# A hybrid decoder trunk: one weight quad loaded in halves, and state products put ahead of their additions

## The chip, the cores and the metric

The kernel runs on one core of a Trainium2 chip. The metric is device time in microseconds (us) of one execution. Before the change the median of 3 runs is 1538.26 us (1537.71 to 1540.48).

## What is computed

The reference runs one inference step of a two-layer trunk for a prompt (256 tokens) and for 8 samples of 8 tokens each that share the weights. A layer is a mixer (state-space heads beside retention heads), a cross-attention on 256 memory tokens, and a mixture of experts. The part that matters here is the mixer's carried state, and the projection of the memory for the attention that follows:

```python
def step(s, inp):                     # ssd_scan, one chunk: states of (heads, 64, 128) per sample
    cs, cd = inp
    return cd[..., None, None] * s + cs, s
y_off = jnp.einsum('bclgn,bcghpn,bclgh->bclghp', Cc, s_in, jnp.exp(a_cum))

def step(s, kv):                      # retention_chunkwise: states of (4, 128, 256) per sample
    return chunk_decay * s + kv, s
o_cross = jnp.einsum('bclhd,bchde->bclhe', q_start, s_in)

mem_k, mem_v = mem @ w_mk, mem @ w_mv # per layer, 256 tokens, 1024 to 1024
```

For the samples the old state s comes from memory, is multiplied by queries (y_off, o_cross), and a new state (decay times old state, plus a product of this step) is returned.

## The kernel before, in words

All weights and old states come through one stream of "quads", arrays of 128 partitions x 4096 floats (2 MB, 16 KB in each partition). SyncE (SP) issues their loads in a fixed order on one queue; each goes into a slot, and in the mixer there are three slots, called ring. A load waits until its slot is freed: `freed[s]` is raised by TensorE (riding on a later matmul) or by VectorE, `loaded[s]` by the landing.

The stage of the diff stands at the end of each layer's mixer. It takes four state quads, k = 0 to 3 (`Q_STATE`: retention, state space, retention, state space; four samples each), between which stand the four quads of memory weights (`Q_MEM`, 16 chunks of 128 columns, four to a quad). The order of the loads there is: second memory quad (chunks 4 to 7), state k = 1, state k = 2, third memory quad (chunks 8 to 11), state k = 3, fourth memory quad. The third memory quad goes into the slot of the second, state k = 3 into that of state k = 1.

TensorE's order is written out by hand. For each k: `from_states(k)` multiplies queries by old states (L860); `new_states(k, 0)` makes what is added to the first half of the new states (L893 for retention, L896 for state space); `project_memory(1)` does one chunk (L613, 16 matmuls); `turn_off(k)` transposes (L872) the result of from_states; then `new_states(k, 1)`. The banks of PSUM into which new_states writes are used again by each half, so a half waits for VectorE's addition of the half before (`s_newst`).

VectorE makes each new state half. For retention one instruction multiplies and adds (L1956). For state space there are two: old state times decay (L1962) and then the addition of the product from PSUM (L1969). Between the halves it scales what TensorE transposes (L1990, state space alone) and adds the transposed result (`add_off`, L1980; `s_offadd` releases from_states of the next k). After the second half it frees the state's slot. A gate product over the prompt (L2007) stands behind k = 0. GpSimd stores each half (1 MB) to memory from one of three buffers; `s_store` guards their reuse. ScalarE copies the memory chunks and the retention part out of PSUM.

Of the kernel before, what the change touches and what calls it, by code (L numbers as in the profile page):

```python
# [20 lines left out]
ALU = mybir.AluOpType  # L21
AX = mybir.AxisListType

P = 128
DEPTH = 2
D = 1024
KD = D // P
# [134 lines left out]
def build(nc, stream, params, consts, x_in, mem_in, y_out, st_out, conv_out, mk_out, mv_out):  # L162
    with ExitStack() as ctx:
# [150 lines left out]

        loaded = [sem(f"s_loaded{s}") for s in range(WIDER)]
        freed = [sem(f"s_freed{s}") for s in range(WIDER)]
        s_slab = [sem(f"s_slab{i}") for i in range(3)]
        s_sq = sem("s_sq")
        s_acc = sem("s_acc")
        s_acc0 = sem("s_acc0")  # L320
# [193 lines left out]
        @block.sync  # L514
        def _(sp):
            sp.dma_start(x[:], x_in).then_inc(s_const, 16)
            sp.dma_start(par[:], params.rearrange("l p n -> p l n")).then_inc(s_const, 16)
            sp.dma_start(cst[:, 0:FIRST], consts[:, 0:FIRST]).then_inc(s_const, 16)
            for L in range(DEPTH):
                for q in range(QUADS):  # L520
                    s, n = slot_of(q), use_of(L, q)
                    if n >= 1:
                        sp.wait_ge(freed[s], n)
                    if q == SLOTS.index(3):
                        for i in range(3):
                            sp.wait_ge(s_store[i], 16 * STORES[i] * (L + 1))
                    if q == SLOTS.index(4):
                        sp.wait_ge(s_ottout, (L + 1) * 4)
                        sp.wait_ge(s_mvstore, 16 * (L + 1))
                    if q == SLOTS.index(6):  # L530
                        sp.wait_ge(s_xs, L * 8 + 6)
                        sp.wait_ge(s_mkstore, 16 * (L + 1))
                    if q == SLOTS.index(7):
                        sp.wait_ge(s_rtok, L + 1)
                        sp.wait_ge(s_quarter, L + 1)
                        sp.wait_ge(s_tstore, 16 * (L + 1))
                    if L + q == 0:
                        for i in range(3):
                            sp.dma_start(slots[s][:, i * SLAB:(i + 1) * SLAB], stream[q][:, i * SLAB:(i + 1) * SLAB])\
                                .then_inc(s_slab[i], 16)  # L540
                        sp.dma_start(slots[s][:, 3 * SLAB:], stream[q][:, 3 * SLAB:]).then_inc(loaded[s], 16)
                    else:
                        sp.dma_start(slots[s], stream[L * QUADS + q]).then_inc(loaded[s], 16)
                    if L == 0 and q == RING - 1:
                        sp.dma_start(cst[:, FIRST:], consts[:, FIRST:]).then_inc(s_tables, 16)
                    if q == RING - 1:
                        if L > 0:
                            sp.wait_ge(freed[6], L * SLOTS.count(6))
                        sp.dma_start(mem, mem_in).then_inc(s_mem, 16)
                sp.wait_ge(s_spilt, L + 1)  # L550
                with sp.If(sp.value_load(spilt[P - 1:P, L:L + 1], min_val=0, max_val=1) > 0):
                    sp.wait_ge(d_start, L * (E + 1) + 1)
                    sp.wait_ge(s_rows, 64 * (L + 1))
                    for t in range(3):
                        sp.dma_start(h_back[0:TOKN[t], t, :], h_rows[L][tok(t), :]).then_inc(d_rows, 16)
                    sp.wait_ge(d_hback, (L + 1) * KD)
                    for e in range(E):
                        sp.wait_ge(d_start, L * (E + 1) + e + 1)
                        q = L * QUADS + Q_MOE + 6 * (e // 2)
                        for m in range(6):  # L560
                            sp.dma_start(all_w[:, m // 2, (m % 2) * 2048:(m % 2 + 1) * 2048]
                                         .rearrange("p (k n) -> p k n", k=2),
                                         stream[q + m].rearrange("p (k a n) -> p k a n", k=2, a=2)[:, :, e % 2, :])\
                                .then_inc(d_loaded, 16)
                with sp.Else():
                    sp.sem_inc(d_loaded, 96 * E)
                    sp.sem_inc(d_rows, 48)
            for i in range(4):
                c = slice(i * KD // 4, (i + 1) * KD // 4)
                sp.wait_ge(s_h, DEPTH * KD + (i + 1) * KD // 4)  # L570
                sp.dma_start(y_out[:, c, :], h[:, c, :]).then_inc(s_ystore, 16)
            sp.wait_ge(s_ystore, 64)
# [3 lines left out]
        def _(pe):  # L576
# [50 lines left out]
            def mixer(L):  # L627
# [9 lines left out]
                def project(q0, chunks, banks=4, src=h, gained=None):  # L637
                    nonlocal n_proj
                    for c in chunks:
                        if L + q0 == 0 and c < 3:  # L640
                            pe.wait_ge(s_slab[c], 16)
                            w = slots[0]
                        else:
                            w = quad(pe, L, q0 + c // 4)
                        if n_proj >= 4:
                            evacuated(n_proj - banks)
                        products(psum[:, n_proj % banks, 0:T], w, (c % 4) * SLAB, P, src, gained).then_inc(s_proj, 1)
                        n_proj += 1
                        if c % 4 == 3:
                            free(q0 + c // 4)  # L650
# [82 lines left out]
                def project_memory(chunks):  # L733

                    nonlocal n_mem
                    for _ in range(chunks):
                        c = n_mem
                        w = quad(pe, L, Q_MEM[c // 4])
                        if 1 <= c < 6:
                            pe.wait_ge(s_mkvout, L * 16 + c)  # L740
                        elif c == 6:
                            pe.wait_ge(s_oout, (L + 1) * 3)
                        elif c > 6:
                            pe.wait_ge(s_mkvout, L * 16 + c - 1)
                        products(memory_out(c), w, (c % 4) * SLAB, P, mem).then_inc(s_mkv, 1)
                        n_mem += 1
                        if c % 4 == 3:
                            free(Q_MEM[c // 4])
# [899 lines left out]
        def _(dve):  # L1648
# [31 lines left out]
            def mixer(L):  # L1680
# [258 lines left out]
                                                     op0=ALU.mult, op1=ALU.add)  # L1939
                        dve.drain().then_inc(s_kvout, 1)  # L1940

                def state_half(k, half):

                    ret, gb = STATES[k]
                    u = 2 * k + half
                    slot = STORE_SLOT[u]
                    ws = batches(ring[:, Q_STATE[k] % RING, :])
                    so = batches(new_of[slot])
                    stores = STORES[slot] * L + (slot == 0) + STORE_SLOT[:u].count(slot)
                    if stores > 0:  # L1950
                        dve.wait_ge(s_store[slot], 16 * stores)
                    if ret:
                        dve.wait_ge(s_batch, L * 8 + u + 1)
                        for i in range(2):
                            r = 2 * half + i
                            dve.scalar_tensor_tensor(out=so[:, :, i * DV:(i + 1) * DV],  # L1956
# [1 line left out]
                                                     in1=psum[:, 0:4, i * DV:(i + 1) * DV],  # L1958
                                                     op0=ALU.mult, op1=ALU.add)
                    else:  # L1960
                        h0 = half * H // G
                        dve.tensor_tensor(so.rearrange("p b (h d) -> p b h d", d=HD),  # L1962
                                          ws[:, :, half * BANK:(half + 1) * BANK]
                                          .rearrange("p b (h d) -> p b h d", d=HD),
                                          last_s[:, h0:h0 + H // G, 4 * gb:4 * gb + 4].rearrange("p h b -> p b h")
                                          .unsqueeze(3).broadcast_to([P, 4, H // G, HD]), ALU.mult)
                        dve.wait_ge(s_batch, L * 8 + u + 1)
                        dve.drain()
                        dve.tensor_tensor(so, so, psum[:, 0:4, :], ALU.add)  # L1969
                    dve.drain().then_inc(s_newst, 1)  # L1970
# [1 line left out]
                def add_off(k):  # L1972
# [8 lines left out]
                                                [:, :, :, 0:DS], ALU.add)  # L1981
                    ins.then_inc(s_offadd, 1)

                dve.wait_ge(s_oout, (L + 1) * 3)
                for k in range(4):
                    ret, gb = STATES[k]
                    quad(dve, L, Q_STATE[k])
                    if not ret:
                        dve.wait_ge(s_off, L * 4 + k + 1)
                        dve.tensor_tensor(off_tok.rearrange("p (g h d) -> p g h d", g=G, h=H // G),  # L1990
                                          psum[:, 5:7, :].rearrange("p g (h d) -> p g h d", h=H // G),
                                          grown[:, gb, :].rearrange("p (g h) -> p g h", g=G).unsqueeze(3)
                                          .broadcast_to([P, G, H // G, HD]), ALU.mult).then_inc(s_offtok, 1)
                    state_half(k, 0)
                    add_off(k)
                    if k == 3:
                        dve.drain()
# [3 lines left out]
                        hg = h[:].rearrange("p (g i) t -> p g i t", g=G)  # L2001
                        dve.tensor_tensor(hg[:, :, 0:2, :], hg[:, :, 0:2, :], hg[:, :, 2:4, :], ALU.add)\
                            .then_inc(s_pair6, 1)
                    state_half(k, 1)
                    dve.drain().then_inc(freed[Q_STATE[k] % RING], 1)
                    if k == 0:
                        dve.tensor_tensor(xbc[:, 0:KD, 0:SEQ], xbc[:, 0:KD, 0:SEQ], zv[:, :, 0:SEQ], ALU.mult)\  # L2007
                            .then_inc(s_gated, 1)

                dve.wait_ge(s_sq6, L * 2 + 2)  # L2010
                hr = h[:].rearrange("p (r i) t -> p r i t", r=RH)
# [445 lines left out]
```

## Time and profile before

| | us |
|---|---|
| median of the runs | 1538.26 |
| the profiled execution's own time | 1539.63 |
| its span | 1537.5 |
| TensorE matmul busy | 1467.1 (95%) |
| VectorE busy | 536.3 (35%) |
| ScalarE busy | 256.6 (17%) |
| mean granted TensorE clock | 0.984 |

The span runs from the first to the last instruction of the program. A busy share is an average over stages of different kinds; whether an engine sets the time is read from the waits in a stage. "Granted clock" is the share of full speed that TensorE was given. "DMA to landing" is the time from the issue of a load to its last byte.

### The profile page before, as it was taken

How to read it: one execution, taken by the hardware profiler on the slowest of the kernel's cores; microseconds unless marked ns; L12 is line 12 of the kernel's file. 1: busy time of each engine (PE TensorE's matmuls, PEld its weight loads, DVE VectorE, ACT ScalarE, POOL GpSimd, SP SyncE). 2: the span in 40 equal slices, each digit the busy share in tenths (PEclk: the TensorE clock that was granted, in tenths of full speed). 3: DMA queues.
4: the chain of work that ended last, by engine and by line, in shares of the span. 5: the costliest groups of instructions: out<-in, count | busy, mean ns of one | idle time of the engine just before them, and what ended most of it. 6: DMA issues, size and time to landing. Idle time of an engine off the chain costs nothing.

```text
span 1537.5 us, 17999 instructions
## 1 busy us (share of the span) xinstructions
PE 1467.1 (95%) x7436; PEld 919.0 (60%) x7436; DVE 536.3 (35%) x1138; ACT 256.6 (17%) x573; POOL 78.4 (5%) x138
## 2 busy tenths in 40 slices
PE   7999899899999999999999998998999999999997
PEld 5776667577766644444467776685777666344443
DVE  3323755571123322222324156546511334122212
ACT  1002321230112210101100132211310112010102
POOL 0000310000000000000000021100000000000000
PEclk9999999899999999999999999998999999999999
DMA  8334432885349789999923343428933696999994
GB/s 330 110 110 165 155 100 91 320 327 196 136 165 403 311 338 427 425 427 427 402 77 142 132 170 103 148 83 320 352 149 110 232 422 256 390 425 427 428 426 186
DMA packets 36102, 397.55 MB, mean 259 GB/s; under 512 B 6214, under 2 KB 6790, under 8 KB 11312
## 3 DMA queue, kind: packets, MB, share of 16 engines
q1 hardware_dynamic: 26192, 358.95, 58.6%
q0 software_dynamic: 9696, 37.13, 6.3%
q8 instruction: 61, 1.00, 0.3%
q10 hardware_dynamic: 128, 0.26, 0.1%
q14 instruction: 25, 0.20, 0.0%
HBM read 370.21 MB, written 27.37 MB: 259 GB/s over the span
## 4 chain that ended last, share of the span: by engine, by line
PE 90%; DVE 3%; DMA 3%; DVEq 1%; ACT 1%; issue 1%; ACTq 0%; SPq 0%
PE psum L613 39%; PE psum L1198 14%; PE psum L953 9%; PE psum L1218 7%; PE psum L1243 5%; DMA ring<-stream 1%; PE psum L620 1%; PE psum L625 1%; PE psum L987 1%; PE psum L1032 1%; PE psum L1050 1%; PE psum L1003 1%; DMA work<-acum_flat 1%; PE psum L1150 1%; PE psum L798 1%; PE psum L1174 1%
## 5 line engine op out<-in xcount | busy, mean ns | idle before, releaser
L613 PE MATMUL psum<-rest,ring 128*128 128x320 f32 x1664 | 456.7, 434 | 0.9 <-issue 0.9
L613 PEld LDWEIGHTS psum<-rest,ring 128*128 128x128 f32 x1664 | 314.5, 190 | 134.5 <-issue 7.4
L613 PE MATMUL psum<-store,ring 128*128 128x256 f32 x512 | 125.9, 403 | 6.4 <-DMA ring<-stream 6.4
L613 PEld LDWEIGHTS psum<-store,ring 128*128 128x128 f32 x512 | 101.5, 202 | 28.9 <-DMA ring<-stream 7.5
L953 PE MATMUL psum<-work,ring 128*128 128x320 f32 x384 | 104.9, 433 | 0.9 <-ACT work L1376 0.9
L953 PEld LDWEIGHTS psum<-work,ring 128*128 128x128 f32 x384 | 72.3, 190 | 30.9 <-ACT work L1376 1.8
L1198 PE MATMUL psum<-ring,work 128*64 128x512 f32 x384 | 86.1, 594 | 0.0
L613 PE MATMUL psum<-work,ring 128*128 128x320 f32 x256 | 72.7, 446 | 11.0 <-DVE work L1661 11.0
L1667 DVE TENSOR_TENSOR x<-x,psum 128x320 f32<-128x320 f32 x32 | 15.6, 488 | 178.7 <-PE psum L953 126.6
L1243 PE MATMUL psum<-work 128*128 128x320 f32 x256 | 76.9, 444 | 0.5 <-issue 0.5
L2144 DVE TENSOR_TENSOR x<-x,psum 128x320 f32<-128x320 f32 x128 | 59.8, 485 | 48.2 <-PE psum L1243 44.6
L2206 DVE TENSOR_TENSOR work<-work,psum 128x512 f32<-128x512 f32 x16 | 11.0, 687 | 175.6 <-ACT work L1610 175.6
L1243 PEld LDWEIGHTS psum<-work 128*128 128x128 f32 x256 | 46.0, 189 | 40.7 <-issue 25.0
L613 PEld LDWEIGHTS psum<-work,ring 128*128 128x128 f32 x256 | 50.2, 197 | 32.8 <-issue 13.8
L1198 PEld LDWEIGHTS psum<-ring,work 128*64 128x64 f32 x384 | 27.0, 137 | 54.1 <-issue 53.5
L1198 PE MATMUL psum<-work 128*64 128x512 f32 x256 | 57.2, 594 | 0.0
L1610 ACT ACTIVATE work<-psum 128x512 f32<-128x512 f32 x16 | 9.6, 597 | 263.1 <-PE psum L1198 263.1
L1349 ACT ACTIVATE rest<-x 128x320 f32<-128x320 f32 x56 | 25.5, 467 | 136.5 <-DVE x L1667 126.4
L2212 DVE COPY work<-psum 128x512 f32<-128x512 f32 x16 | 11.1, 691 | 100.8 <-PE psum L1218 100.8
L1396 ACT ACTIVATE work<-psum 128x256 f32<-128x256 f32 x24 | 9.2, 385 | 220.9 <-PE psum L613 220.9
L1218 PE MATMUL psum<-ring,work 128*64 128x512 f32 x192 | 43.4, 594 | 1.4 <-ACT work L1612 1.4
L1732 DVE SCALAR_TENSOR_TENSOR work<-work,par 128x344 f32<-128x344 f32 x72 | 41.5, 576 | 5.4
(314 smaller groups left out, 1536.8 us busy)
## 6 DMA issues: line engine op xcount, KB each, us to landing
ring<-stream SPq DMA_DIRECT2D x99, 2048.0 KB, 10.7
work<-stream SPq DMA_DIRECT2D x24, 2048.0 KB, 21.4
states_out<-stream SPq DMA_DIRECT2D x20, 2048.0 KB, 13.8
store<-stream SPq DMA_DIRECT2D x12, 2048.0 KB, 17.7
rest<-stream SPq DMA_DIRECT2D x12, 2048.0 KB, 20.3
st_out<-states_out POOLq DMA_DIRECT2D x12, 1024.0 KB, 11.1
st_out<-work POOLq DMA_DIRECT2D x6, 1024.0 KB, 7.9
work<-acum_flat POOLq DMA_DIRECT2D x10, 256.0 KB, 4.0
```

The costliest lines, as they stand in the source:

```text
L613: mm = pe.matmul(out, w[:, a:a + P], rhs[:, j, :], start=(j == 0), stop=(j == KD - 1))
L620: mm = pe.transpose(o, i, ident[0:i.shape[0], 0:i.shape[0]])
L625: return pe.transpose(out[0:TOKN[t], :], src[:, tok(t)], ident)
L798: mm = pe.matmul(o, x_of[t][:, hd * HD:(hd + 1) * HD], dec[:, 0, hh * n:(hh + 1) * n], start=True, stop=(t != 1), skip_group_check=True)
L953: mm = pe.matmul(psum[:, j % 4, 0:T], w[:, a:a + P], src, start=(i == 0), stop=(i == 15))
L1198: mm = pe.matmul(psum[ab * CAP:(ab + 1) * CAP, up, :], h_packed[:, p % 2, k, ab * CAP:(ab + 1) * CAP], w[:, a:a + BANK], start=(k == 0), s ...
L1218: mm = pe.matmul(psum[ab * CAP:(ab + 1) * CAP, 2 + half, :], hidden_t[:, f, ab * CAP:(ab + 1) * CAP], w[:, a:a + BANK], start=(f == 0), st ...
L1243: pe.matmul(psum[:, SPREAD[j], 0:T], y_pair[:, j * P:(j + 1) * P], picked_ts[p % 4], start=True, stop=True).then_inc(s_spread, 1)
L1349: act.activation(dst, x[:, j, :], ACT.Square, scale=D ** -0.5).then_inc(s_sq, 1)
L1667: dve.tensor_tensor(x[:, j, :], x[:, j, :], psum[:, j % 4, 0:T], ALU.add).then_inc(s_xadd, 1)
L1732: ins = dve.scalar_tensor_tensor(out=a, in0=raw[:, c, j:j + XOUT], scalar=par[:, L, wa + j:wa + j + 1], in1=a, op0=ALU.mult, op1=ALU.add)
L2144: dve.tensor_tensor(x[:, j, :], x[:, j, :], psum[:, SPREAD[j], 0:T], ALU.add)\
```

## The change

SP loads the third memory quad in two halves. The first half (chunks 8 and 9) waits only until chunk 5 has been projected, so that the columns of chunks 4 and 5 in the slot are done with; the second half waits for the slot as before. TensorE takes chunks 8 and 9 when the first half is there. The three semaphores of the very first load, `s_slab`, are renamed `s_piece`, and the first of them is used for the new half as well.

On VectorE `state_half` is split. `kept_states` holds the wait for the store buffer and, for state space, the product of old states; `added_states` the wait for TensorE's new states, the addition, and retention's single instruction. The product of a half now stands ahead of the scaling (L1990) or of add_off, and the gate product ahead of the whole stage. The bytes, matmuls and VectorE instructions are the same in number and size; there is one more load instruction per layer.

```diff
                 for q in range(QUADS):
                     s, n = slot_of(q), use_of(L, q)
+                    if q == Q_MEM[2]:
+                        sp.wait_ge(s_mkv, L * 16 + 6)
+                        sp.dma_start(slots[s][:, 0:2 * SLAB], stream[L * QUADS + q][:, 0:2 * SLAB])\
+                            .then_inc(s_piece[0], 16)
+                        sp.wait_ge(freed[s], n)
+                        sp.dma_start(slots[s][:, 2 * SLAB:], stream[L * QUADS + q][:, 2 * SLAB:])\
+                            .then_inc(loaded[s], 16)
+                        continue
...
-                        w = quad(pe, L, Q_MEM[c // 4])
+                        if c in (8, 9):
+                            pe.wait_ge(s_piece[0], 16 * (L + 2))
+                            w = slots[slot_of(Q_MEM[2])]
+                        else:
+                            w = quad(pe, L, Q_MEM[c // 4])
...
-                def state_half(k, half):
+                def kept_states(k, half):
...
+                    if not ret:
+                        h0 = half * H // G
+                        dve.tensor_tensor(batches(new_of[slot]).rearrange("p b (h d) -> p b h d", d=HD),
...
+                def added_states(k, half):
...
+                    dve.wait_ge(s_batch, L * 8 + u + 1)
...
+                dve.tensor_tensor(xbc[:, 0:KD, 0:SEQ], xbc[:, 0:KD, 0:SEQ], zv[:, :, 0:SEQ], ALU.mult)\
+                    .then_inc(s_gated, 1)
                 dve.wait_ge(s_oout, (L + 1) * 3)
                 for k in range(4):
                     ret, gb = STATES[k]
                     quad(dve, L, Q_STATE[k])
+                    kept_states(k, 0)
                     if not ret:
...
-                    state_half(k, 0)
+                    added_states(k, 0)
+                    if k < 3:
+                        kept_states(k, 1)
                     add_off(k)
...
-                    state_half(k, 1)
+                    if k == 3:
+                        kept_states(k, 1)
+                    added_states(k, 1)
                     dve.drain().then_inc(freed[Q_STATE[k] % RING], 1)
-                    if k == 0:
-                        dve.tensor_tensor(xbc[:, 0:KD, 0:SEQ], xbc[:, 0:KD, 0:SEQ], zv[:, :, 0:SEQ], ALU.mult)\
-                            .then_inc(s_gated, 1)
```

What it does to the order. First VectorE in layer 0, from the first half of k = 0 to the end of k = 1, before (the gate product is the row with 128x8x256, s_loaded0 is the load of state quad k = 1, s_batch the new states from TensorE):

```order
L1956 SCALAR_TENSOR_TENSOR work<-ring,psum 128x4x256 [waits s_batch,s_loaded1,s_oout]
L1980 TENSOR_TENSOR work<-work,psum 128x4x32 [waits s_offt]
L1956 SCALAR_TENSOR_TENSOR states_out<-ring,psum 128x4x256 [waits s_batch,s_store0]
L2007 TENSOR_TENSOR work<-work 128x8x256
L1990 TENSOR_TENSOR rest<-psum,grown 128x1024 [waits s_off,s_loaded0]
L1962 TENSOR_TENSOR states_out<-ring,rest 128x2048
L1969 TENSOR_TENSOR states_out<-states_out,psum 128x2048 [waits s_batch]
L1980 TENSOR_TENSOR work<-work,psum 128x4x32 [waits s_offt]
L1962 TENSOR_TENSOR work<-ring,rest 128x2048 [waits s_store2]
L1969 TENSOR_TENSOR work<-work,psum 128x2048 [waits s_batch]
```

The same stretch of VectorE after the change:

```order
L2001 TENSOR_TENSOR work<-work 128x8x256
L1980 SCALAR_TENSOR_TENSOR work<-ring,psum 128x4x256 [waits s_batch,s_loaded1,s_oout]
L1997 TENSOR_TENSOR work<-work,psum 128x4x32 [waits s_offt,s_store0]
L1980 SCALAR_TENSOR_TENSOR states_out<-ring,psum 128x4x256 [waits s_batch]
L1964 TENSOR_TENSOR states_out<-ring,rest 128x2048 [waits s_loaded0]
L2010 TENSOR_TENSOR rest<-psum,grown 128x1024 [waits s_off]
L1986 TENSOR_TENSOR states_out<-states_out,psum 128x2048 [waits s_batch]
L1964 TENSOR_TENSOR work<-ring,rest 128x2048 [waits s_store2]
L1997 TENSOR_TENSOR work<-work,psum 128x4x32 [waits s_offt]
L1986 TENSOR_TENSOR work<-work,psum 128x2048 [waits s_batch]
```

The gate product went to the front, the product of k = 1, half 0, took its place ahead of the scaling, and that of half 1 went ahead of add_off, with its wait for a store. Now SP's loads in the same stage of layer 0, before: state k = 1 (s_freed0), state k = 2, third memory quad, state k = 3, fourth memory quad.

```order
L543 DMA ring<-stream 128x4096 [waits s_freed0]
L543 DMA ring<-stream 128x4096 [waits s_freed1]
L543 DMA ring<-stream 128x4096 [waits s_freed2]
L543 DMA ring<-stream 128x4096 [waits s_freed0]
L543 DMA ring<-stream 128x4096 [waits s_freed1]
```

The same loads after the change:

```order
L551 DMA ring<-stream 128x4096 [waits s_freed0]
L551 DMA ring<-stream 128x4096 [waits s_freed1]
L524 DMA ring<-stream 128x2048 [waits s_mkv]
L527 DMA ring<-stream 128x2048 [waits s_freed2]
L551 DMA ring<-stream 128x4096 [waits s_freed0]
L551 DMA ring<-stream 128x4096 [waits s_freed1]
```

The first half (s_mkv) no longer waits for the slot, and it still stands behind the load of state k = 2 on the one queue.

## Rows read from the trace of the kernel before

**Rows 1.** Page: the chain that ended last, by engine.

```profile
PE 90%; DVE 3%; DMA 3%; DVEq 1%; ACT 1%; issue 1%; ACTq 0%; SPq 0%
```

**Rows 2.** Waits of TensorE (us, times, longest), first layer 0, then layer 1.

```profile
PE psum L613 <- DMA ring<-stream: 2.7, 1, 2.7
PE psum L893 <- DVEq L1970: 2.2, 1, 2.2
PE psum L896 <- DVEq L1970: 0.9, 2, 0.5
...
PE psum L613 <- DMA ring<-stream: 3.7, 1, 3.7
PE psum L896 <- DVEq L1970: 1.2, 2, 0.7
```

**Rows 3.** Timeline, layer 0: start, us, engine, line, out<-in, [idle before <-releaser].

```profile
272.31 1.15 PE L893 MATMUL psum<-states_out 8*128 8x256 f32 x16
273.63 2.35 DVE L1956 SCALAR_TENSOR_TENSOR work<-ring,psum 128x1024 f32<-128x1024 f32 x2 [7.34 <-PE psum L893]
281.76 2.29 DVE L2007 TENSOR_TENSOR work<-work 128x2048 f32<-128x2048 f32 x1 [0.21 <-issue]
288.19 2.29 DVE L1969 TENSOR_TENSOR states_out<-states_out,psum 128x2048 f32<-128x2048 f32 x1
290.56 1.14 PE L896 MATMUL psum<-rest 8*128 8x512 f32 x8 [0.42 <-DVEq L1970]
291.00 2.28 DVE L1962 TENSOR_TENSOR work<-ring,rest 128x2048 f32<-128x2048 f32 x1
293.36 2.29 DVE L1969 TENSOR_TENSOR work<-work,psum 128x2048 f32<-128x2048 f32 x1
295.73 1.96 PE L893 MATMUL psum<-work 8*128 8x256 f32 x16 [2.19 <-DVEq L1970]
300.42 6.54 PE L613 MATMUL psum<-store,ring 128*128 128x256 f32 x16 [2.73 <-DMA ring<-stream]
309.10 1.90 PE L860 MATMUL psum<-ring,work 128*8 128x512 f32 x16 [0.19 <-DMA ring<-stream]
312.55 3.72 PE L613 MATMUL psum<-store,ring 128*128 128x256 f32 x16
```

**Rows 4.** Timeline, layer 1: from_states of k = 2 and k = 3.

```profile
1053.54 3.51 PE L860 MATMUL psum<-ring,rest 128*8 128x256 f32 x32 [0.78 <-DMA ring<-stream]
1070.12 1.90 PE L860 MATMUL psum<-ring,work 128*8 128x512 f32 x16
```

**Rows 5.** SP's load line: issues and times to landing, layer 0, then layer 1.

```profile
L543 SPq DMA_DIRECT2D ring<-stream x3: 328/328/328, 281.7 to 295.8; - x3
289.41 0.33 SPq L543 DMA_DIRECT2D ring<-stream  x1
DMA to landing us min/median/max: 9.4/11.0/13.3
...
L543 SPq DMA_DIRECT2D ring<-stream x3: 327/327/327, 1042.8 to 1056.9; - x3
DMA to landing us min/median/max: 10.7/11.3/12.2
```

**Rows 6.** DMA issues, 281.6 to 296 us: KB each, median us to landing.

```profile
st_out<-states_out POOLq DMA_DIRECT2D x2, 1024.0 KB, 11.8
```

**Rows 7.** DMA queues (packets, MB, share): 304 to 306, then 27 to 28 us.

```profile
q1 hardware_dynamic: 34, 0.56, 64.9%
q0 software_dynamic: 32, 0.26, 30.9%
...
q1 hardware_dynamic: 51, 0.41, 98.4%
```

**Rows 8.** Windows: us, busy by engine, granted clock, DMA share, GB/s.

```profile
300.40:306.10 5.70, 5.68 (x13) 4.54 (x14) 0.00 (x0) 0.00 (x0) 0.53 (x1) 0.50 1.01 428
1053.70:1057.00 3.30, 3.30 (x36) 1.06 (x28) 2.93 (x2) 0.70 (x1) 0.00 (x0) 0.50 0.98 350
```

More of the change, by code:

```diff
@@ L316, in build @@
         freed = [sem(f"s_freed{s}") for s in range(WIDER)]
-        s_slab = [sem(f"s_slab{i}") for i in range(3)]
+        s_piece = [sem(f"s_piece{i}") for i in range(3)]
         s_sq = sem("s_sq")
@@ L539, in _ @@
                             sp.dma_start(slots[s][:, i * SLAB:(i + 1) * SLAB], stream[q][:, i * SLAB:(i + 1) * SLAB])\
-                                .then_inc(s_slab[i], 16)
+                                .then_inc(s_piece[i], 16)
                         sp.dma_start(slots[s][:, 3 * SLAB:], stream[q][:, 3 * SLAB:]).then_inc(loaded[s], 16)
@@ L640, in project @@
                         if L + q0 == 0 and c < 3:
-                            pe.wait_ge(s_slab[c], 16)
+                            pe.wait_ge(s_piece[c], 16)
                             w = slots[0]
@@ L1946, in state_half @@
                     slot = STORE_SLOT[u]
-                    ws = batches(ring[:, Q_STATE[k] % RING, :])
-                    so = batches(new_of[slot])
                     stores = STORES[slot] * L + (slot == 0) + STORE_SLOT[:u].count(slot)
@@ L1951, in state_half @@
                         dve.wait_ge(s_store[slot], 16 * stores)
+                    if not ret:
+                        h0 = half * H // G
+                        dve.tensor_tensor(batches(new_of[slot]).rearrange("p b (h d) -> p b h d", d=HD),
+                                          batches(ring[:, Q_STATE[k] % RING, :])[:, :, half * BANK:(half + 1) * BANK]
+                                          .rearrange("p b (h d) -> p b h d", d=HD),
+                                          last_s[:, h0:h0 + H // G, 4 * gb:4 * gb + 4].rearrange("p h b -> p b h")
+                                          .unsqueeze(3).broadcast_to([P, 4, H // G, HD]), ALU.mult)
+                def added_states(k, half):
+                    ret, gb = STATES[k]
+                    u = 2 * k + half
+                    ws = batches(ring[:, Q_STATE[k] % RING, :])
+                    so = batches(new_of[STORE_SLOT[u]])
+                    dve.wait_ge(s_batch, L * 8 + u + 1)
                     if ret:
-                        dve.wait_ge(s_batch, L * 8 + u + 1)
                         for i in range(2):
@@ L1960, in state_half @@
                     else:
[L1961 to L1967, printed above, removed]
                         dve.drain()
```

## The prediction

> **What bounds the kernel now.** I first read the chain of waits: TensorE holds 90% of it [rows 1]. A microsecond counts only where TensorE waits or runs slowly, so I asked next what TensorE waits for in the stage that the diff touches (255 to 345 us in layer 0, 1016 to 1106 in layer 1). In layer 0 these are 2.7 us for a load before a memory chunk (L613), 2.2 us for VectorE before the new states of k = 2 (L893), and 0.5 us, the longest of two waits, before those of k = 3 (L896); in layer 1 they are 3.7 and 0.7 us [rows 2]. The timeline then shows the place: chunk 8, the first of the third memory quad, starts at 300.42 and takes 6.54 us instead of the 3.72 of chunk 9 at 312.55, and the products with the last state quad (k = 3, L860) start at 309.10, released by a DMA after only 0.19 us of waiting [rows 3]. So two loads end almost together there: the memory quad is late, and the last state quad is as late as the work that the memory quad delayed. In layer 1 the same products start at 1070.12 with no wait for a load shown [rows 4].
>
> I name the loads A (state quad of k = 2), B (third memory quad) and C (state quad of k = 3). SP issues them from 281.7 to 295.8, B at 289.41; their times to landing run from 9.4 over 11.0 to 13.3 us [rows 5], and 289.41 + 11.0 = 300.4 and 295.8 + 13.3 = 309.1 are the starts of chunk 8 and of L860. So A lands at 291.1. In layer 1 A is issued at 1042.8 and C at 1056.9 and the times are 10.7, 11.3 and 12.2 [rows 5]: A lands at 1053.5, C at 1069.1.
>
> **VectorE's part.** The gate product (2.29 us at 281.76) goes ahead of the stage, into the 7.34 us in which VectorE waits before 273.63 [rows 3]: cost nothing. In its old slot now stands the product of k = 1, half 0 (L1962, 2.28 us). The addition of that half (L1969, 2.29 us at 288.19) therefore starts 2.28 us earlier, at 285.9, and ends at 288.2. The second product (2.28 us) then runs to 290.5, and the second addition needs new states from TensorE (L896 at 290.56), which no longer wait 0.42 us for VectorE and end at 290.56 - 0.42 + 1.14 = 291.3 [rows 3]. The addition ends at 293.6 instead of 293.36 + 2.29 = 295.65. That is worth 2.0 us: the 2.2 us wait at 295.73 almost goes, and C, which SP issues 0.15 us behind that addition, goes out at 293.8 instead of 295.8. The waits for stores (s_store) that now stand ahead of add_off hold up only add_off and what is behind it on VectorE, which is TensorE's k = 3 through s_offadd. A store takes about 11.8 us to land [rows 6], so the one of k = 1, half 0, issued at 288.4, is there at about 300 to 302, before C. I take nothing for them; if C came early they would be next.
>
> **The load's part.** Half of B is issued right behind A, since chunk 5 stands on TensorE ahead of the new states on which A's release rests. Behind A on the same queue, its 1.05 MB land between 293.6 (all 0.41 MB/us for it) and 296.3 (half of that). TensorE asks for chunk 8 at about 294.9 (new states from 293.7, 1.15 us for L893 at full clock [rows 3]). So the 2.7 us wait goes or shrinks to about 1.4, chunk 8 ends by 303 even at its slow 6.54 us, and the rest of k = 2 (transposes and new states, 309.10 - 306.96 = 2.1 us) by 305. TensorE then wants C. What is late next is C, and the question is when C lands.
>
> **When C lands.** In 304 to 306 us the load queue moved 34 packets, 0.56 MB, and the store queue 32 packets, 0.26 MB [rows 7]: one packet each in turn, a load's 16 KB (a row of a whole quad) against a store's 8 KB, so 0.28 and 0.13 MB/us, 0.41 together. Half a quad has rows of 8 KB; a load with such rows, alone, moved 51 packets in 0.41 MB [rows 7]. One for one against stores, it gets half, 0.205 MB/us. No row shows 8 KB loads beside stores; the bounds are this half and the old two thirds, 0.28.
> Here a rule helps. The rows show equal packet counts; the Trainium skill (DMA: Bandwidth & Descriptors, Queues, rings and completion order) states that an engine "round-robins between the queue rows it has work for, at packet granularity". By it the halves get the equal share, and by a share fixed in bytes they would keep two thirds.
> From A's landing, B (2.10 MB) at 0.205 takes 10.2 us and C at 0.28 takes 7.5: C lands at 291.1 + 17.7 = 308.8, and in layer 1 at 1053.5 + 17.7 = 1071.2. With two thirds for both, 15.0 us: 306.1 and 1068.5. With no store in the way, 2 x 2.10 / 0.41 = 10.2 us: 301.3 and 1063.7. Stores have nearly always work there, since VectorE now ends its halves earlier; for small gaps between them I take 0.6 us off the first case: 308.2 and 1070.6. Against the starts of L860 at 309.10 and 1070.12 that is -0.9 and +0.5 us. The gain of the early half is thus mostly returned: the queue is not idle between A and C any more, but B takes its turns in smaller pieces.
>
> **The clock.** TensorE now stands from about 302 to 305 until C, 3 to 6 us. Waits of 2.7 and 3.7 us in before were followed by a granted clock of 0.50, the level of 1.2 GHz, for the 5.7 us from 300.40 and for the 3.3 us from 1053.70 [rows 8]; L860 took 3.51 us there [rows 4] against 1.90 [rows 3]. Half of such a time is lost, 1.6 to 2.9 us; I take 2.0 per layer, nearer to L860's own 1.6. In before the slow stretch lay on chunk 8, where in layer 0 the wait for C covered it. On the other side the waits of 0.5 and 0.7 us at L896 go [rows 2], since VectorE is through with k = 2 before C lands.
>
> **Sum.** Layer 0: -0.9 + 2.0 - 0.5 = +0.6. Layer 1: +0.5 + 2.0 - 0.7 = +1.8. Together +2.4 us. Behind this stage the chain is TensorE's again, so the shift is carried to the end as it is. The profiled execution took 1539.63 us (1537.5 of span and 2.1 around it) and would take 1542.0; the median of the runs is 1.4 lower, so I predict 1538.3 + 2.4 = 1540.7 us. A difference below 0.2% (3.1 us) can't be told from no change.
>
> **Rivals.**
> 1. C comes early enough. For it: A's, B's and C's packets now follow without the gaps at the starts of B and C, and C is issued 2.0 us earlier. With two thirds of the bytes C starts L860 at 306.1 and 1068.5: -3.0 and -1.6, with the same clock terms (+2.0 - 0.5, +2.0 - 0.7) -1.8 in all, 1536.5; with no loss of clock -5.8, 1532.5. With stores out of the way TensorE, not C, decides, at about 302 and 1064: -7 and -6, 1525. Against it: the equal packet counts. Chance 0.22, of which 0.03 for the last.
> 2. Slower: the long wait for C costs the clock over chunk 9 too. Place: L860 to chunk 9 of k = 3; price: half of 5.7 us per layer, 2.9, with C at 308.8 and 1071.2 (no gaps between stores): (-0.3 + 2.9 - 0.5) + (1.1 + 2.9 - 0.7) = +5.4, 1543.7. It decides as soon as TensorE waits for C more than about 4 us and the halves get only half. For it: the 5.7 us row; against it: the 3.3 us row. Chance 0.30.
> 3. The change doesn't do what it says: half of B is issued only after A on SP's one queue, and if B's landing hardly moves, only the clock's place changes. Then chunk 8 starts at 300 as now and C at 309: 1538. Chance 0.05.
> The forecast has the remaining 0.43.
>
> **How the numbers follow.** The forecast's own range is 1538.5 to 1542. For 8 in 10 I reach to 1534.0 in rival 1 (C early with part of the clock kept) and to 1544.5 in rival 2. Faster by over 0.2% (below 1535.2): most of the parts of rival 1 without clock loss and with stores away, 0.14, and 0.04 for a forecast off on both landings: 0.18. Slower (above 1541.3): rival 2 with 0.27 and the upper end of the forecast with 0.10: 0.37. Within 0.2%: 0.45.
>
> **What would show it.** Right: chunk 8 starts at 295 to 297, and L860 of k = 3 is released by a DMA after a wait of 3 us or more, within 1.5 us of 309 and 1070, with a granted clock of 0.5 behind it; C's time to landing grows to 14 us or more from an issue at about 293.8; the gate product stands ahead of 273. Wrong: L860 of k = 3 starts before 306, or the wait for C is below 1 us, or the packets of the two queues in 292 to 299 stand two to one in bytes.

## The result and the profile after

The changed kernel took 1542.1 us (median of 19 runs, 1538.7 to 1546.0), the kernel before 1539.2 (19 runs, 1537.2 to 1543.6): a ratio of 1.0018, 95% interval 1.001 to 1.0027. It is slower by about 2.9 us, where 2.4 was forecast. The profiled execution of the changed kernel took 1538.73 us, the least of its 19, and 0.9 us less than the profiled execution of the kernel before; times of the stage are therefore compared within the traces, from the start of the stage on.

The two profiled executions also differ at places that the diff doesn't touch. The same 32 products far behind the stage in layer 1, after the same wait of 1.10 us, before and after the change:

```profile
1297.09 6.56 PE L1150 MATMUL psum<-work 128*128 128x128 f32 x32 [1.10 <-DVE work L2135]
...
1298.58 3.81 PE L1162 MATMUL psum<-work 128*128 128x128 f32 x32 [1.10 <-DVE work L2156]
```

The granted clock there was 0.55 and 1.00; in layer 0 the same products took 6.61 and 5.44 us. One such place is worth nearly as much as the whole effect, so whether the change costs time is read from the 19 runs of each kernel, and the traces tell only where.

The waits of TensorE after the change, layer 0 and then layer 1 (us in all, times, longest), against [rows 2]:

```profile
PE psum L872 <- DMA ring<-stream: 6.0, 1, 6.0
PE psum L621 <- DMA ring<-stream: 1.3, 1, 1.3
PE psum L905 <- DVEq L1987: 0.6, 1, 0.6
...
PE psum L872 <- DMA ring<-stream: 6.3, 2, 5.3
PE psum L621 <- DMA ring<-stream: 1.9, 1, 1.9
```

The wait for VectorE before the new states shrank from 2.2 to 0.6 us, the 0.5 and 0.7 us before those of k = 3 are gone, and the wait for chunk 8 shrank from 2.7 and 3.7 to 1.3 and 1.9. A new wait of 6.0 and 5.3 us stands before the products with the last state quad (L872, which was L860). The timeline shows it, layer 0 against [rows 3], layer 1 against [rows 4]:

```profile
263.58 1.78 PE L621 MATMUL psum<-store,ring 128*128 128x256 f32 x7
266.66 2.29 DVE L2001 TENSOR_TENSOR work<-work 128x2048 f32<-128x2048 f32 x1
...
291.61 2.29 DVE L1986 TENSOR_TENSOR work<-work,psum 128x2048 f32<-128x2048 f32 x1 [0.32 <-PE psum L908]
296.39 5.40 PE L621 MATMUL psum<-store,ring 128*128 128x256 f32 x16 [1.27 <-DMA ring<-stream]
...
309.79 3.60 PE L872 MATMUL psum<-ring,work 128*8 128x512 f32 x16 [6.05 <-DMA ring<-stream]
...
314.44 3.72 PE L621 MATMUL psum<-store,ring 128*128 128x256 f32 x16
...
1024.07 2.21 PE L621 MATMUL psum<-store,ring 128*128 128x256 f32 x9
1070.40 3.60 PE L872 MATMUL psum<-ring,work 128*8 128x512 f32 x16 [5.34 <-DMA ring<-stream]
1075.33 3.72 PE L621 MATMUL psum<-store,ring 128*128 128x256 f32 x16
```

The gate product is early (266.66), VectorE's second addition of k = 1 starts at 291.61 instead of 293.36, chunk 8 at 296.39 instead of 300.42. At L872 all of that is gone. Chunk 9, the first of the work behind it, starts at 314.44. The stage begins with chunk 4; in the kernel before its rows, and that of chunk 9 in layer 1, are (some rows of chunks stop where the window that was read stops, so only their starts are used):

```profile
263.33 1.99 PE L613 MATMUL psum<-store,ring 128*128 128x256 f32 x8
...
1024.39 1.78 PE L613 MATMUL psum<-store,ring 128*128 128x256 f32 x7
...
1073.84 1.35 PE L613 MATMUL psum<-store,ring 128*128 128x256 f32 x5
```

From chunk 4 to chunk 9 it was 312.55 - 263.33 = 49.22 us in layer 0 and 49.45 in layer 1; now it is 314.44 - 263.58 = 50.86 and 1075.33 - 1024.07 = 51.26. That is 1.64 and 1.81 us longer, 3.45 in all, inside what the runs give (1.5 to 4.2 us by the interval of the ratio).

The loads of layer 0 as SP issues them (start, us) are those of A, of B's halves and of C; below them stands C's time to landing (15.8 in layer 1):

```profile
281.89 0.33 SPq L551 DMA_DIRECT2D ring<-stream  x1
282.26 0.43 SPq L524 DMA_DIRECT2D ring<-stream  x1
289.66 0.33 SPq L527 DMA_DIRECT2D ring<-stream  x1
294.04 0.33 SPq L551 DMA_DIRECT2D ring<-stream  x1
...
DMA to landing us min/median/max: 15.7/15.7/15.7
```

C lands at 294.04 + 15.7 = 309.7, hardly later than before (309.1), though it is issued 1.8 us earlier. What the two queues moved between A's landing and C's in layer 0 (packets, MB, share; q1 is the load queue, q0 the store queue), before (291.1 to 309.1) and after the change (291.5 to 309.7):

```profile
q1 hardware_dynamic: 288, 4.19, 63.3%
q0 software_dynamic: 388, 2.79, 36.9%
...
q1 hardware_dynamic: 440, 4.46, 57.8%
q0 software_dynamic: 481, 3.42, 44.6%
```

The store queue got 0.6 MB more ahead of C than before, and 0.8 MB more in layer 1 (3.23 against 2.41). Most of it in layer 0 went where the store queue had been empty, from 292 to 295 us, before and after:

```profile
q1 hardware_dynamic: 56, 0.92, 90.4%
q0 software_dynamic: 1, 0.01, 0.6%
...
q1 hardware_dynamic: 90, 0.74, 57.9%
q0 software_dynamic: 84, 0.56, 44.1%
```

Before, B had the engines to itself there. The windows after (us, busy by engine, granted clock, DMA share, GB/s), first the stretch from A to C in layer 0, then the one behind the wait, against [rows 8]:

```profile
291.50:309.70 18.20, 10.39 (x88) 7.33 (x88) 7.47 (x7) 3.38 (x3) 1.59 (x3) 0.82 1.03 434
...
306.70:313.40 6.70, 3.61 (x20) 0.52 (x20) 2.29 (x1) 0.00 (x0) 0.31 (x1) 0.50 1.00 424
```

The DMA engines are full from A's landing to C's, at 434 GB/s; before it was 389 in layer 0 (7.00 MB in 18.0 us). The DMA share was 1.01 before too, so it doesn't tell the two apart; the bytes do. Of the 0.9 MB that moved in addition, 0.6 were stores.

### The profile page after: what moved, and what is told of

Its sections match the earlier page's. It is cut to its first block, busy times and chain, and to the rows that moved or that the text cites. A ratio compares the mean times of both kernels' runs of the same rounds, so it can differ in the third digit from the quotient of the medians.

```text
span 1536.6 us, 18000 instructions
## 1 busy us (share of the span) xinstructions
PE 1461.0 (95%) x7436; PEld 913.6 (59%) x7436; DVE 536.6 (35%) x1138; ACT 256.3 (17%) x573; POOL 78.5 (5%) x138
## 4 chain that ended last, share of the span: by engine, by line
PE 88%; DMA 5%; DVE 3%; ACT 1%; DVEq 1%; issue 1%; ACTq 0%; SPq 0%
PE psum L621 39%; PE psum L1210 13%; PE psum L965 9%; PE psum L1230 7%; PE psum L1255 5%; DMA ring<-stream 5%; PE psum L628 1%; PE psum L633 1%; PE psum L999 1%; PE psum L1044 1%; PE psum L872 1%; PE psum L1062 1%; PE psum L1015 1%; DMA work<-acum_flat 1%; PE psum L810 1%
## 5 line engine op out<-in xcount | busy, mean ns | idle before, releaser
L1679 DVE TENSOR_TENSOR x<-x,psum 128x320 f32<-128x320 f32 x32 | 15.6, 487 | 178.7 <-PE psum L965 126.6
## 6 DMA issues: line engine op xcount, KB each, us to landing
states_out<-stream SPq DMA_DIRECT2D x20, 2048.0 KB, 14.1
store<-stream SPq DMA_DIRECT2D x12, 2048.0 KB, 18.7
ring<-stream SPq DMA_DIRECT2D x4, 1024.0 KB, 13.4
```

The costliest lines, as they stand in the source:

```text
L1679: dve.tensor_tensor(x[:, j, :], x[:, j, :], psum[:, j % 4, 0:T], ALU.add).then_inc(s_xadd, 1)
```

## The experiments

Each ran beside the kernel before on its chip; ratios are to that. "Behind A" is C's landing less A's, 18.0 us in layer 0 and 15.6 in layer 1 before, 18.3 and 17.5 after the change.

**VectorE's order alone** (the changed kernel without the half loads):

```diff
-                    if q == Q_MEM[2]:
-                        sp.wait_ge(s_mkv, L * 16 + 6)
...
-                        continue
```

> Only VectorE's new order; the third memory quad (B) is loaded whole, as before. Theory (the time is set by when the last state quad C lands, and the halves of B make it no earlier): B lands about as before (chunk 8 at about 300 in layer 0), C is issued 2 us earlier and lands within 1 us of 309, no long wait of TensorE ahead of C: the kernel before within 1.5 us, ratio 0.999 to 1.001. Rival (VectorE's waits for stores, now ahead of add_off, cost the 2.9 us): ratio about 1.002, with TensorE waiting for s_offadd at k = 3.

Ratio 1.0015 (0.9998 to 1.0031). The trace shows chunk 8, and the queues from 292 to 295 us:

```profile
301.84 6.00 PE L613 MATMUL psum<-store,ring 128*128 128x256 f32 x16 [6.97 <-DMA ring<-stream]
...
q1 hardware_dynamic: 35, 0.57, 47.9%
q0 software_dynamic: 74, 0.61, 47.7%
```

B is a whole quad again, and it is the late one: 12.4 us from issue to landing where it took 11.0, with a wait of 7.0 us that the theory did not have. VectorE's earlier additions start the stores earlier: 0.61 MB in these 3 us instead of 0.01, and 3.11 MB between A and C instead of 2.79. C, issued 2 us earlier, lands 18.0 us behind A as before (17.0 in layer 1, where it was 15.6); L860 of k = 3 follows the work behind chunk 8, at 309.72, without waiting for C. So the order alone already feeds the stores, without any half.

**Half loads alone** (the kernel before, with the half loads and TensorE's wait for them):

```diff
+                    if q == Q_MEM[2]:
+                        sp.wait_ge(s_mkv, L * 16 + 6)
...
+                        continue
```

> Only the two half loads; VectorE in the order of before. Theory: chunk 8 starts at 296 to 297 in layer 0, C is issued at about 295.8 and still lands at 309 to 310, TensorE waits for it 5 us or more and runs L860 of k = 3 at half clock: 2 to 4 us slower than before, ratio 1.0013 to 1.0026, all of the change's loss. Rival (VectorE's order costs it): no slower than before, ratio 1.000 or less.

Ratio 0.9993 (0.9973 to 1.0012): no loss that can be told, and its interval holds neither the forecast loss nor the 1.0018 of the whole change, whose own interval overlaps it. C is issued at 295.88 as before and lands 17.3 and 17.0 us behind A. In layer 0 TensorE waits 2.7 us for it, in layer 1 6.4 us with half clock behind:

```profile
308.61 1.90 PE L872 MATMUL psum<-ring,work 128*8 128x512 f32 x16 [2.71 <-DMA ring<-stream]
...
1070.76 3.60 PE L872 MATMUL psum<-ring,work 128*8 128x512 f32 x16 [6.38 <-DMA ring<-stream]
```

The wait has moved to L872 here too, but the time does not say that this alone costs anything. From 292 to 295 us the store queue moved 0.19 MB here, against 0.61 with the order alone.

**Few stores** (the changed kernel; each store of a new state writes 256 of 2048 columns, so most of that output is left out):

```diff
-                    pool.dma_start(st_out[L, 1 + u], new_of[STORE_SLOT[u]]).then_inc(s_store[STORE_SLOT[u]], 16)
+                    pool.dma_start(st_out[L, 1 + u][:, 0:256], new_of[STORE_SLOT[u]][:, 0:256]).then_inc(s_store[STORE_SLOT[u]], 16)
```

> The changed kernel in which each of the eight stores of new states per layer writes only its first 256 of 2048 columns, so most of those outputs are left out. Theory (C lands late because the stores take turns with the loads): nearly alone the loads run at about 0.41 MB/us, C lands about 10 to 12 us behind A instead of 17.5 to 18.3, TensorE hardly waits for it and keeps its clock: 6 to 9 us less per layer than the changed kernel, ratio to before 0.990 to 0.994. Rival (the extra load instruction and the late issue of C set its landing, not the stores): C 15 us or more behind A, ratio 1.000 to 1.002.

Ratio 0.9918 (0.9894 to 0.9942). C takes 9.3 and 8.1 us from issue to landing and is 13.4 and 12.3 behind A; the wait for it is 2.7 and 1.5 us:

```profile
303.12 3.57 PE L872 MATMUL psum<-ring,work 128*8 128x512 f32 x16 [2.71 <-DMA ring<-stream]
```

With the issues unchanged, the stores alone move C by about 5 us per layer. The products still ran at a slow clock (3.57 us in layer 0, 2.68 in layer 1), where the theory had them keep it.

**State k = 3 ahead of the second half** (the changed kernel, order of two loads):

```diff
-                        sp.wait_ge(freed[s], n)
-                        sp.dma_start(slots[s][:, 2 * SLAB:], stream[L * QUADS + q][:, 2 * SLAB:])\
-                            .then_inc(loaded[s], 16)
...
+                    if q == Q_STATE[3]:
+                        m = Q_MEM[2]
+                        sp.wait_ge(freed[slot_of(m)], use_of(L, m))
+                        sp.dma_start(slots[slot_of(m)][:, 2 * SLAB:], stream[L * QUADS + m][:, 2 * SLAB:])\
+                            .then_inc(loaded[slot_of(m)], 16)
```

> The changed kernel with C issued ahead of the second half of B, which chunk 10 needs only after k = 3 has begun. Theory: the second half no longer stands in C's way, 1.05 MB at 0.21 MB/us are 5 us; C, issued at 294.0, lands 3 to 5 us earlier (305 to 306.5 in layer 0), TensorE waits 1 to 3 us instead of 6; per layer 3 to 5 us less than the changed kernel, that is 1532 to 1536 where before is 1539: ratio 0.995 to 0.998. Rival (a fixed cost of one more load, or stores alone, decide C's landing): C within 1 us of 309.5, ratio 1.001 to 1.002. The second half then lands at about 310 to 311, ahead of chunk 10 at 314.

Ratio 0.9947 (0.993 to 0.9965). C takes 11.6 and 11.2 us to land, 14.4 and 12.8 behind A; the wait is 2.2 us in both layers:

```profile
307.74 3.03 PE L874 MATMUL psum<-ring,work 128*8 128x512 f32 x16 [2.21 <-DMA ring<-stream]
...
312.72 6.61 PE L623 MATMUL psum<-store,ring 128*128 128x256 f32 x16
```

Here L874 is the line of L872. With 1 MB less ahead of C the loss turns into a gain. The slow clock reached chunk 9 in this execution (6.61 us).

**Loads with rows of 4 KB** (the changed kernel, B in four loads of one chunk each):

```diff
+                        for i in range(4):
+                            if i == 0:
+                                sp.wait_ge(s_mkv, L * 16 + 6)
+                            if i == 2:
+                                sp.wait_ge(freed[s], n)
+                            sp.dma_start(slots[s][:, i * SLAB:(i + 1) * SLAB],
...
```

> The changed kernel with the third memory quad loaded in four pieces of one chunk each, rows of 4 KB instead of 8 KB, the first two at once where the half was, the last two where the second half was. Theory (one packet each in turn, so a load with smaller rows gets a smaller share beside stores of 8 KB): B's last piece lands 2 to 5 us later than the second half did and C 2 to 4 us later, 20 us or more behind A; 2 to 4 us per layer slower than the changed kernel, ratio to before 1.004 to 1.007. Rival (shares go by bytes, whatever the packets): C as in the changed kernel, 17.5 to 18.5 us behind A, ratio 1.001 to 1.003.

Ratio 1.0036 (1.0019 to 1.0053). C lands 21.4 and 18.1 us behind A, after 18.7 us from its issue in layer 0. The row of L872 (L874 here), and the queues from 294 to 297 us, with B alone on the load queue:

```profile
312.62 3.60 PE L874 MATMUL psum<-ring,work 128*8 128x512 f32 x16 [12.06 <-DMA ring<-stream]
...
q0 software_dynamic: 106, 0.81, 64.0%
q1 hardware_dynamic: 125, 0.45, 36.5%
```

Where both queues have work, the smaller rows get about half as many bytes as the stores. Over 291.3 to 302 us it is 2.17 MB against 2.24, since the store queue is nearly empty in between (0.02 MB from 292 to 293 us, 0.04 from 297 to 298). Layer 1 moved little (18.1 against 17.5).

**Stores with rows of 4 KB** (the changed kernel, each store in two of 0.5 MB):

```diff
-                    pool.dma_start(st_out[L, 1 + u], new_of[STORE_SLOT[u]]).then_inc(s_store[STORE_SLOT[u]], 16)
+                    for i in range(2):
+                        pool.dma_start(st_out[L, 1 + u][:, i * 1024:(i + 1) * 1024],
+                                       new_of[STORE_SLOT[u]][:, i * 1024:(i + 1) * 1024])\
+                            .then_inc(s_store[STORE_SLOT[u]], 16)
```

> The changed kernel, but GpSimd stores each half of a new state as two stores of 0.5 MB with rows of 4 KB, where it was one of 1 MB with rows of 8 KB; the same bytes in all. Theory (the two queues take turns row by row, so a smaller row of the stores leaves more to the loads): beside a store the halves of the third memory quad get two thirds (8 to 4) and state k = 3 four fifths (16 to 4, 0.33 of 0.41 MB/us); 2.1 MB of halves take about 7.7 us instead of 10.2 and 2.1 MB of state k = 3 about 6.4 instead of 7.5, so state k = 3 lands 14 to 16 us behind state k = 2 (18.3 and 17.5 in the changed kernel), TensorE waits for it 1 to 4 us instead of 6.05 and 5.34, and the time is 0.992 to 0.999 of the kernel before. Rival 1 (the shares don't go by rows): state k = 3 lands 17 to 19 us behind and the time is that of the changed kernel, 1.001 to 1.003. Rival 2 (stores that last longer cost more elsewhere: VectorE waits for a buffer, and the twice as many issues on GpSimd delay others): state k = 3 lands earlier, but VectorE's waits for stores grow by microseconds and the time is 1.002 or more.

Ratio 0.9963 (0.9945 to 0.9982). C takes 11.6 us instead of 15.7 and lands 15.3 and 14.5 us behind A, 3.0 less than in the changed kernel in both layers. But TensorE's wait stays at 5.8 and 5.2 us: chunk 8 no longer waits for its half and TensorE asks for k = 3 earlier, and VectorE ends the wait. The queues from 299.2 to 300.8 us, VectorE's add_off of k = 2 (L1997), and L872:

```profile
q1 hardware_dynamic: 37, 0.61, 91.0%
q0 software_dynamic: 33, 0.12, 18.2%
...
305.99 0.48 DVE L1997 TENSOR_TENSOR work<-work,psum 128x128 f32<-128x128 f32 x2 [7.18 <-DMA st_out<-states_out]
...
306.62 3.60 PE L872 MATMUL psum<-ring,work 128*8 128x512 f32 x16 [5.79 <-DVE work L1997]
```

The store buffer of `kept_states(2, 1)` comes free late, and that wait now stands ahead of add_off, which releases the products of k = 3. It is the smaller part: C landed at 305.8 (294.15 + 11.6) and in layer 1 at 1066.1, so the store holds TensorE 0.8 and 1.3 us longer than C does, and the rest of the wait is still C's. The theory was right on C and on the time and wrong on the wait (1 to 4 us); the second rival's wait for stores was there, but not its time.

**TensorE kept at work while it waits** (20 products without use before those of k = 3):

```diff
+                    if k == 3:
+                        for _ in range(20):
+                            pe.matmul(psum[:, 4, 0:M], ident, mem[:, 0, :], start=True, stop=True)
```

> The changed kernel with 20 matmuls of 128x256 more (about 4.7 us at full clock, their result is never read) ahead of from_states of k = 3, where TensorE waits for C. Theory (half of L860's time there is the clock's): L860 of k = 3 takes 1.9 instead of 3.6 us at a granted clock of 1.0, C lands as in the changed kernel; 1.5 to 2 us per layer less than it, about before + 0 (ratio 0.9990 to 1.0005). Rival (the clock is not part of the loss): ratio stays at 1.0018, or rises.

Ratio 1.0011 (0.9994 to 1.0027): inconclusive as a time. The added products took 8.90 us (the profile counts 40 matmuls for the 20 written), longer than the wait:

```profile
305.64 8.90 PE L917 MATMUL psum<-store,cst 128*128 128x256 f32 x40
314.47 1.90 PE L872 MATMUL psum<-ring,work 128*8 128x512 f32 x16
...
305.70:314.40 8.70, 8.70 (x42) 7.46 (x40) 4.64 (x3) 0.00 (x0) 0.53 (x1) 1.00 1.01 429
```

C landed at 311.9 (15.7 us after its issue at 296.2), so the filler overran it by 2.6 us, more than the 1.7 that the full clock gave back. The clock part is plain: granted 1.00, and L872 in 1.90 us instead of 3.60. It was the same in layer 1 (L872 at 1076.14, 1.90 us): with no idle time ahead of them, the products had the full clock in both layers.

**Chunk 9 ahead of the products of k = 3** (the changed kernel; ScalarE's copies are reordered to match):

```diff
                 for k in range(4):
+                    if k == 3:
+                        project_memory(1)
                     from_states(k)
...
-                memory(2)
+                memory(3)
```

> The changed kernel with chunk 9, whose columns land with the first half of B, moved on TensorE ahead of from_states of k = 3, and ScalarE's copy of chunk 10 ahead of its wait for the transposes. Loads and VectorE as in the changed kernel. Theory (what is lost is TensorE's wait for C and the clock that goes with it, not C's landing itself): C lands as late as before, 17 to 18.5 us behind A, but TensorE waits for it only 1 to 3 us instead of 6 and runs L860 of k = 3 mostly at full clock: 4 to 6 us less per layer than the changed kernel, ratio to before 0.994 to 0.997. Rival (what follows on VectorE and ScalarE, the scaling and transposes behind from_states of k = 3, is the limit): the wait turns up behind from_states, ratio 1.000 to 1.002.

Ratio 0.9933 (0.9913 to 0.9954). C lands as in the changed kernel, 18.5 and 17.1 behind A, and the wait is 2.55 and 2.85 us. L872 and chunk 10 behind it:

```profile
310.21 3.05 PE L872 MATMUL psum<-ring,work 128*8 128x512 f32 x16 [2.55 <-DMA ring<-stream]
...
315.20 6.60 PE L621 MATMUL psum<-store,ring 128*128 128x256 f32 x16
```

Chunk 9's data lie there already; doing it inside the wait takes some 3.7 us of work [rows 3] out of what follows. The clock part of the theory failed: a wait is left, and L872 took 3.05 and 3.16 us behind it, chunk 10 6.60 in layer 0. The gain is a little more than was expected all the same; the profiled execution, the slowest of its six, doesn't show where that comes from.

**Both** (state k = 3 ahead of the second half, and chunk 9 early):

> Chunk 9 early and C issued ahead of the second half of B. Theory: C lands 13 to 14.5 us behind A, about when chunk 9 ends, so nothing is left of the wait for it; chunk 10 then waits 1 to 3 us for the second half (it landed at 312.6 in layer 0 with C first). Per layer 5 to 7 us less than the changed kernel, ratio to before 0.993 to 0.996; no better than chunk 9 early alone by more than 2 us per layer.

Ratio 0.9907 (0.9887 to 0.9926), 1528.4 us, better than the 0.993 to 0.996 that was expected. C lands 14.1 and 13.1 us behind A, and the products of k = 3 need no wait and have the full clock, here in layer 0 (1.90 us in layer 1 too):

```profile
310.03 1.90 PE L874 MATMUL psum<-ring,work 128*8 128x512 f32 x16
```

**Both, and stores with rows of 4 KB**:

> State k = 3 loaded ahead of the second half, chunk 9 ahead of the wait for it (0.991 of the kernel before), and the stores of new states in two pieces with rows of 4 KB. Theory (turns row by row): state k = 3 lands 11 to 12.5 us behind state k = 2 instead of 14.1 and 13.1, but TensorE already waited for it at most 1.0 us, so little is left to win: 0.988 to 0.992. The second half lands earlier too, 13 us from its issue instead of about 16. Rival (the stores, held back, become late themselves): VectorE waits for store buffers, and the time is 0.993 or more.

Ratio 0.9902 (0.9873 to 0.9931), 1526.4 us; it can't be told from the version before it, as the theory said: TensorE waits 0.9 and 0.4 us for C. But C landed 14.9 and 14.2 us behind A, later than the 11 to 12.5 of the theory, and the second half took 14.5 us instead of 13; what held them is open. Both versions beat both kernels of this study.

## Why the prediction was right, and where it was off

The mechanism that the prediction gave is the one that the traces show, and its time, 1540.7 from 1538.3, lies near the measured +2.9 us.

- **VectorE ahead by 2 us: held.** The second addition ended at 291.61 + 2.29 = 293.9 (said: 293.6), C was issued at 294.04 (293.8), and the gate product cost nothing. The wait before the new states shrank to 0.6 us.
- **Chunk 8 early: held.** 296.39, at the end of the 294.9 to 296.3 given for the landing of the half; it kept 1.3 us of its wait and its slow clock.
- **C late: held in its cause, one size off.** The halves' rows share about evenly with the stores: from 291 to 293 us, with only the halves on the load queue, the trace has (2.02 to 1.81 MB from 291 to 300)

```profile
q1 hardware_dynamic: 58, 0.46, 54.1%
q0 software_dynamic: 51, 0.41, 48.3%
```

and for C from 300 to 307 us two to one in bytes again:

```profile
q1 hardware_dynamic: 143, 2.08, 69.4%
q0 software_dynamic: 134, 0.97, 32.7%
```

The counts of packets lie near each other (they include some under 512 B, 30 of these last 277), and the bytes follow the rows. This agrees with the rule that the prediction took from the Trainium skill (DMA: Bandwidth & Descriptors, Queues, rings and completion order), as far as counts can show it: a packet of that page holds several descriptors, a packet of the profile here is one row. That the share matters to the time is shown from both sides by the loads of 4 KB (C 3.1 us later in layer 0) and the stores of 4 KB (C 3.0 us earlier behind A in both layers). The size that was off is the 0.6 us taken off C for gaps between stores: the stores had work all the way from A to C (3.42 MB), and C came 18.3 and 17.5 us behind A. The working without gaps gives 17.7; the other 0.6 us in layer 0 stay open.
- **What the prediction gave no price.** It put C's delay on the rows of the halves, and only named that VectorE now ends its halves earlier. That alone brought more stores ahead of C (3.11 MB against 2.79, and 0.60 more in the 3 us in which the store queue had been empty). By the timed runs it may be the larger part of the loss, 1.0015 against 0.9993 for the halves, but both intervals hold 1; in the profiled executions the stage grew by 1.25 us with the order alone and by 1.71 with the halves alone (1.13 less in layer 0, 2.84 more in layer 1). How the loss divides stays open.
- **The clock: held, smaller than taken.** Granted 0.50 behind the wait; L872 took 3.60 instead of 1.90 us, so 1.7 per layer, and in layer 1 0.3 more at L908 (1.47 against 1.14), for the 2.0 taken. Chunk 9 ran in 3.72 us in both layers: rival 2 did not happen in this execution, though the waits of 6.05 and 5.34 us were longer than the 4 us that it asked for. The slow clock did reach that chunk in the kernel with state k = 3 first, behind a wait of 2.21 us. The profiled execution was the fastest of its 19, and no trace tells what the clock did in the others.
- **The sum.** Layer 0, from the start of the stage: L872 +0.44 (309.79 - 309.10, less the 0.25 by which the stage began later), +1.70 clock, -0.5 for the gone wait: +1.64, where +0.6 was said. Layer 1: +0.60, +1.70 + 0.33, -0.7: 1.9, where the rows show +1.81 and +1.8 was said. The error of the sum, about 1 us, lies in layer 0: C 1.3 us later than said, the clock 0.3 us cheaper.
- **Stores that hold add_off: rightly costed at nothing, with its condition.** "If C came early they would be next" is what the kernel with stores of 4 KB shows: at L1997 a store ends 7.18 us of idle time, and TensorE starts 0.8 us behind C's landing. Rival 1, that C comes early enough, needed exactly what few stores, or another order of the loads, supply.

## What to carry to other kernels

When the DMA engines are full, as here at 434 GB/s, an earlier issue need not bring an earlier landing (C went out 1.8 us earlier and came 0.6 us later): before splitting a load or starting a store earlier, add up the bytes of all queues between the last landing and the load that is needed next, and put loads in the order in which they are needed. In these runs a load and a store that shared the engines moved about as many rows each, so the load split into rows of 4 KB gave some of its share to the stores of 8 KB (0.45 against 0.81 MB in 3 us). And where a wait stays, move work whose data are there into it. That saves the work's time; the full clock came back only where hardly any wait was left (1.90 us with both changes, 3.05 with chunk 9 early alone).

## What was not expected of the hardware

- The throughput between A and C rose when stores stood beside the loads all the way: 434 GB/s after, 389 before. From 292 to 295 us, with the load of B nearly alone, it was 309 before; after the change it was 431 there. Most of the rise went to stores that nothing waited for.
- In the changed kernel the products ran at half clock after 6.05 us of idle, as they did after 2.71 us with few stores; with half loads alone, 2.71 us of idle at 308.61 was followed by the full clock (1.90 us). The 32 products of L1150 ran at 0.55 and at 1.00 behind the same 1.10 us. The length of the wait alone does not tell, and these runs don't settle what does.
